# Stacking a query's high and low parts on the rows of one tile in a latent attention

## What is computed

```python
q = (q_lat @ w_qb).reshape(bsz, t_len, 6, 192)       # 128 plain and 64 rotated per head
q_pe, k_pe = rope_2d(q_pe, cos, sin), rope_2d(k_pe, cos, sin)
k_pe = jnp.broadcast_to(k_pe[:, :, None, :], (bsz, t_len, 6, 64))   # one rotated key for all heads
q, k = jnp.concatenate([q_nope, q_pe], -1), jnp.concatenate([k_nope, k_pe], -1)
s = jnp.einsum('bqhd,bkhd->bhqk', qblk, k) * 192 ** -0.5   # 128 queries against 256 + 512 keys
o = jnp.einsum('bhqk,bkhd->bqhd', jax.nn.softmax(s, axis=-1), v)
```

## Time and profile before

| | |
|---|---|
| median of 3 runs | 2432.0 us (2430.31 to 2433.66) |
| the profiled execution | 2423.83 us, span 2421.7 us |
| mean granted TensorE clock | 0.982 |
| TensorE (PE) busy | 2311.4 us, 95% of the span |
| weight loads (PEld) | 1932.8 us, 80% |
| VectorE (DVE) | 1170.0 us, 48% |
| ScalarE (ACT) | 868.9 us, 36% |
| GpSimd (POOL) | 974.8 us, 40% |
| slowest group of loads to land | 20.9 us (arena<-ada_dram, 768 KB each) |

### The profile page before, as it was taken

One profiled execution on the slowest core, in us unless ns is written; L12 is line 12 of the kernel. 1 busy time (PEld: TensorE's weight loads), 2 busy tenths in 40 slices (PEclk: granted clock), 3 DMA queues, 4 the chain that ended last, 5 costly groups with the idle time before them and its releaser, 6 DMA issues.

```text
span 2421.7 us, 36690 instructions
## 1 busy us (share of the span) xinstructions
PE 2311.4 (95%) x14013; PEld 1932.8 (80%) x14013; DVE 1170.0 (48%) x1873; ACT 868.9 (36%) x1399; POOL 974.8 (40%) x770
## 2 busy tenths in 40 slices
PE   6989989999999999999999999999999999999997
PEld 3878879888888888898877787778887886688766
DVE  4685681547777753343232346654232006670273
ACT  5444343341111122335224343222443225542452
POOL 2464563333333432333512145655664440154302
PEclk9989989999999999999999999999999999999999
DMA  7131232126555531112200024553223321122212
GB/s 287 66 115 69 72 122 84 53 93 203 183 196 191 184 104 61 61 61 91 64 1 1 18 87 156 183 197 110 98 89 116 97 87 47 55 76 90 66 45 70
DMA packets 64438, 245.11 MB, mean 101 GB/s; under 512 B 7168, under 2 KB 8448, under 8 KB 63552
## 3 DMA queue, kind: packets, MB, share of 16 engines
q1 hardware_dynamic: 64080, 242.67, 29.0%
q0 software_dynamic: 240, 0.79, 0.1%
HBM read 241.33 MB, written 2.10 MB: 101 GB/s over the span
## 4 chain that ended last, share of the span: by engine, by line
PE 73%; DVE 4%; issue 3%; ACT 3%; POOL 2%; DVEq 0%; POOLq 0%; ACTq 0%
PE ps L851 13%; PE ps L852 13%; PE ps L853 13%; PE ps L1554 4%; PE ps L1556 4%; PE ps L1557 4%; PE ps L612 2%; PE ps L1802 1%; PE ps L1789 1%; PE ps L1726 1%; POOL w_low L469 1%; PE ps L888 1%; PE ps L890 1%; PE ps L889 1%; ACT arena L2302 1%
## 5 line engine op out<-in xcount | busy, mean ns | idle before, releaser
L469 POOL TENSOR_TENSOR w_low<-ring,w_high 128x512 fp32r<-128x512 f32 (+2 forms) x534 | 752.0, 1430 | 1138.8 <-ACT w_high L460 1132.3
L460 ACT ACTIVATE w_high<-ring 128x1024 fp32r<-128x1024 f32 (+2 forms) x267 | 274.7, 1031 | 957.1 <-PE ps L853 638.8
L851 PE MATMUL ps<-h_high,w_high 128*128 128x512 f32 x1040 | 412.0, 396 | 17.1 <-POOL h_low L714 7.3
L852 PE MATMUL ps<-h_low,w_high 128*128 128x512 f32 x1040 | 407.4, 392 | 0.0
L853 PE MATMUL ps<-h_high,w_low 128*128 128x512 f32 x1040 | 407.0, 391 | 0.0
L851 PEld LDWEIGHTS ps<-h_high,w_high 128*128 128x128 f32 x1040 | 196.6, 189 | 70.9 <-issue 13.2
L853 PEld LDWEIGHTS ps<-h_high,w_low 128*128 128x128 f32 x1040 | 196.4, 189 | 41.7
L852 PEld LDWEIGHTS ps<-h_low,w_high 128*128 128x128 f32 x1040 | 196.8, 189 | 38.0
L2839 DVE TENSOR_TENSOR hidden<-arena,hidden 128x1536 fp32r<-128x1536 f32 (+1 forms) x42 | 87.2, 2077 | 193.3 <-ACT hidden L2098 193.3
L1554 PE MATMUL ps<-hidden,w_high 128*128 128x512 f32 (+1 forms) x504 | 178.6, 354 | 0.0
L1556 PE MATMUL ps<-hidden,w_high 128*128 128x512 f32 (+1 forms) x504 | 178.5, 354 | 0.0
(11 more groups left out here) (465 smaller groups left out, 4868.6 us busy)
## 6 DMA issues: line engine op xcount, KB each, us to landing
const<-late_w_dram SPq DMA_DIRECT2D x112, 512.0 KB, 5.0
ring<-up_dram SPq DMA_DIRECT2D x88, 512.0 KB, 3.3
ring<-down_dram SPq DMA_DIRECT2D x44, 512.0 KB, 3.2
ring<-winE_dram SPq DMA_DIRECT2D x32, 512.0 KB, 3.5
XB<-ada_dram SPq DMA_DIRECT2D x20, 768.0 KB, 5.4
ring<-win_dram SPq DMA_DIRECT2D x20, 512.0 KB, 3.2
ring<-winC_dram SPq DMA_DIRECT2D x20, 512.0 KB, 3.5
arena<-ada_dram SPq DMA_DIRECT2D x12, 768.0 KB, 20.9
```

Source lines behind the costliest of these rows:

```text
L460: nc.scalar.activation(WH[p][:, 0:L], RAW[p][:, 0:L], ACT.Copy).then_inc(w_hi, 1)
L469: ins = nc.gpsimd.tensor_tensor(WL[p][:, to], RAW[p][:, to], WH[p][:, to].bitcast(F32), ALU.subtract)
L851: nc.tensor.matmul(bank[:, 0:n], wh[:, cols], hi, start=(k == 0), stop=False)
L852: nc.tensor.matmul(bank[:, 0:n], wh[:, cols], lo, start=False, stop=False)
```

## The change

The high parts and the low parts of a head's rotated query (64 rows each) are put on the 128 rows of one tile, M_TS[h]: the head's own half of the rows holds the high part, the other half its low part. As the rotated key stands in both halves, one product of that tile with M_RH gives high x high + low x high, and a second with M_RL gives high x low (+ low x low, which was left out before). So `m_scores` issues two rotated products with 128 rows in place of three with 64.

To fill the tiles ScalarE copies the pair's rotated query whole into the first head's tile and its upper half into the second head's; GpSimd makes the low part in place over the query (M_TLOW stands where M_QP does), and SP moves each head's low half to the other half of the rows by a transfer from SBUF to SBUF, 64 rows of 2 KB. SP waits for GpSimd's count before each, and TensorE waits for the transfer (`rot_in[h]`) before each unit. SP issues these six after the first two loads of `woutM`; the other six loads follow.

```diff
--- before.py
+++ after.py
@@ -270,9 +270,10 @@
         M_KH = [parts(f"key_high{x}", at, T) for x, at in enumerate((ARENA_AT + 3072, ARENA_AT))]
         M_KL = [parts(f"key_low{x}", at, T) for x, at in enumerate((H_AT + 3072, ARENA_AT + T))]
         M_RH, M_RL = (parts(f"key_rot{x}", ARENA_AT + 24320 + x * T, T) for x in range(2))
-        M_TH, M_TL = ([parts(f"query_rot{x}{j}", at, S) for j, at in enumerate(ats)] for x, ats in enumerate((
-            (H_AT + KT * S, H_AT + KT * S + 2 * S, ARENA_AT + 24320 + 2 * T),
-            (H_AT + KT * S + S, H_AT + KT * S + 3 * S, ARENA_AT + 24320 - 2 * S))))
+        M_TS = [parts(f"query_rot{h}", at, S) for h, at in enumerate((
+            H_AT + KT * S, H_AT + KT * S + S, H_AT + KT * S + 2 * S, H_AT + KT * S + 3 * S,
+            ARENA_AT + 24320 + 2 * T, ARENA_AT + 24320 - 2 * S))]
+        M_TLOW = [parts(f"query_rot_low{x}", ARENA_AT + 11 * S + 3 * T + x * S, S) for x in range(3)]
         GS = parts("hidden", H_AT, 2, 2, 2, T)
         G1 = [(parts("hidden_first0", ARENA_AT + 32 * T, 2, T), SQR.rearrange("p k n -> p (k n)")[:, 0:2 * T].rearrange("p (k n) -> p k n", k=2)),
               [parts(f"hidden_first1{x}", ARENA_AT + 22 * S + x * 2 * S, 2, S) for x in range(2)]]
@@ -1099,9 +1100,10 @@
                 return M_KN[:, x, :], M_KH[x % 2], M_KL[x % 2]
             if what == "q":
                 return M_QN[:, x, :], SQR[:, 2 * (x % 2), :], SQR[:, 2 * (x % 2) + 1, :]
-            return M_QP[:, x, :], M_TH[x], M_TL[x]
+            return M_QP[:, x, :], M_TS[2 * x:2 * x + 2], M_TLOW[x]
 
         m_tab = sem("m_tab")
+        rot_in = [sem(f"rot_in{h}") for h in range(HEADS_M)]
         m_dft = sem("m_dft")
         m_rope = sem("m_rope")
         m_max = sem("m_max")
@@ -1305,7 +1307,14 @@
                 if stage in LATER:
                     load_up(stage)
                     continue
-                first = 2 if stage in ("woutE", "woutC") else 0
+                first = 2 if stage in ("woutE", "woutC", "woutM") else 0
+                if stage == "woutM":
+                    for k in range(2):
+                        load_split(sp, stage, k, k)
+                    for h in range(HEADS_M):
+                        sp.wait_ge(qk_lo, M_PARTED.index(("t", h // 2)) + 1)
+                        mine, other = slice(64 * (h % 2), 64 * (h % 2) + 64), slice(64 - 64 * (h % 2), 128 - 64 * (h % 2))
+                        sp.dma_start(M_TS[h][other, :].bitcast(F32), M_TLOW[h // 2][mine, :].bitcast(F32)).then_inc(rot_in[h], 16)
                 if stage == "winE":
                     with sp.Fori(0, 4) as i:
                         for k in range(2):
@@ -1693,21 +1702,19 @@
                 h, i = units[u]
                 b = bank_use("mS", u)[0]
                 open_bank(pe, "mS", u)
-                o = 64 * (h % 2)
                 pe.wait_ge(qk_lo, max(M_PARTED.index(x) for x in (("q", h), ("t", h // 2))) + 1)
+                pe.wait_ge(rot_in[h], 16)
                 _, kh, kl = m_parts("k", h)
                 _, qh, ql = (x[:, i * P:(i + 1) * P] for x in m_parts("q", h))
-                _, th, tl = (x[o:o + 64, i * P:(i + 1) * P] for x in m_parts("t", h // 2))
-                rh, rl = M_RH[o:o + 64, :], M_RL[o:o + 64, :]
+                both = M_TS[h][:, i * P:(i + 1) * P]
                 MM = nc.tensor.matmul
                 for j, (a, n) in enumerate(SEGS):
                     to = ps[:, b + j, 0:n]
                     MM(to, qh, kh[:, a:a + n], start=True, stop=False)
                     MM(to, ql, kh[:, a:a + n], start=False, stop=False)
                     MM(to, qh, kl[:, a:a + n], start=False, stop=False)
-                    MM(to, th, rh[:, a:a + n], start=False, stop=False)
-                    MM(to, tl, rh[:, a:a + n], start=False, stop=False)
-                    ins = MM(to, th, rl[:, a:a + n], start=False, stop=True)
+                    MM(to, both, M_RH[:, a:a + n], start=False, stop=False)
+                    ins = MM(to, both, M_RL[:, a:a + n], start=False, stop=True)
                 sums_done(ins, "mS", u)
 
             def m_turn(u):
@@ -2235,7 +2242,11 @@
                             await_sums(act, "mS", 4 * x - 5)
                         await_taken(act, *spread_sum("nqk", 10 + 2 * x if what == "k" else x))
                     whole, high, _ = m_parts(what, x)
-                    A(high, whole, ACT.Copy).then_inc(qk_hi, 1)
+                    if what == "t":
+                        A(high[0], whole, ACT.Copy)
+                        A(high[1][64:128, :], whole[64:128, :], ACT.Copy).then_inc(qk_hi, 1)
+                    else:
+                        A(high, whole, ACT.Copy).then_inc(qk_hi, 1)
 
             part_keys(0, 4)
             for u in range(26):
@@ -2461,6 +2472,7 @@
                     for x in range(len(M_PARTED)):
                         whole, high, low_ = m_parts(*M_PARTED[x])
                         pool.wait_ge(qk_hi, x + 1)
+                        high = high[0] if M_PARTED[x][0] == "t" else high
                         TT(low_, whole, high.bitcast(F32), ALU.subtract).then_inc(qk_lo, 1)
                     continue
                 if stage[:4] == "down":
```

## The result

The changed kernel took 2402.2 us (median of 4 runs, 2399.4 to 2409.6) against 2432.4 us before (4 runs): ratio 0.988, 95% interval 0.986 to 0.990. In more rounds on one chip it took 2403.4 us (6 runs) against 2430.4 (17 runs): ratio 0.989, interval 0.9865 to 0.9915. So it is faster by 27 to 30 us, and by somewhat more than the range of the forecast, 2405 to 2418, allowed.

The account below looks back on a forecast made before the run. TensorE's queue was taken to bound the 24 units: 24 x 0.99 = 23.8 us (8.6 removed product, 15.1 gaps) less 2.7 for stalls at the start gives 21.1 off the 2432.0 median: 2411 us, range 2405 to 2418.

Parts of the forecast that it names:

- The gaps: TensorE's scores: 0.63 us a unit lost at four places where 128-row and 64-row products meet; all go, 15.1 us.
- The added wait: TensorE's wait for the transfer before each unit: 0 to 0.07 us each, 0 to 1.7 in all, taken as 0.
- The three stalls at the start: TensorE waits of 0.6, 0.9 and 1.2 us in the first units, sum 2.7 us given back once.
- (a): Rival: the gaps in the scores aren't the change of shape; 7.6 us less, 2424; 6 in 100.
- (b): Rival: stalls at the start let TensorE's clock fall, costing 0.9 to 1.8 us, 2413; 8 in 100.
- (c): Rival: TensorE no longer bounds the steady part, ScalarE's round does; 6 us, 2417; 9 in 100.
- (d): Rival: slower, as head 0's transfer lands late before the first score product; 2439 if it takes 40 us; 2 in 100.
- New scores: 1.87 us, 0.99 less: Score products of one unit on TensorE after the change: 1.87 us instead of 2.86; over 24 units 23.8 us.
- the 0.08 in front of the transposes: Fourth gap, from the last score product (L1710) to the transposes: 0.20 us for 0.12, counted within the 0.63 us.
- I take the saving off the median: Last step: 21.1 us taken off the timed runs' median 2432.0, though the profiled execution took 2423.8; gives 2411.
- spread of the runs (1.7 to either side): Run-to-run spread added to the bounds 2406.5 and 2416.7 to give the range 2405 to 2418.
- the clock as a rival: Rival (b): the changed kernel's stalls at the start lower the clock, costing 0.9 to 1.8 us; 8 in 100.

Follow-up runs that it names:

- shape alone: Three rotated products as in the kernel before the change, but all with 128 rows (the third repeats the second): 2411.4 us, ratio 0.9935 against that kernel.

## Why the forecast missed

The parts that were right, by its own steps. The gaps belong to the change of shape (shape alone). The products that stay take no longer with 128 rows. SP, GpSimd and the transfers cost nothing, with 1253.1 for the first low half, as against 1253.2, and a landing in 2.4 us. The added wait cost nothing in the stage and 0.1 us in front of it. The three stalls at the start were forecast as 0.6, 0.9 and 1.2 and are 0.71, 0.91 and 1.17. Rivals (a), (b), (c) and (d) did not happen; the stalls at the start left the clock at 1.00.

**A term too small.** "New scores: 1.87 us, 0.99 less" is 1.84 and 1.02: the plain step with 512 columns is 0.23, not the 0.24 that I read from one unit. And I named the 0.08 in front of the transposes as a gap but took back no gain in the transposes' own first step; it is 0.06. So 25.9 (24 x 1.08) less 2.8 is 23.1, and measured 22.7, where I had 23.8 less 2.7, 21.1. Most of the 0.4 between lies behind the start of the last unit, where the changed kernel gains 0.9 us instead of 1.2.

**The step that failed** is the last one, "I take the saving off the median", with its "spread of the runs (1.7 to either side)". It made the saving of one undisturbed profile the saving of every execution. The term that it put at nothing is what the 64-row form in head 0 costs in executions where the clock falls: 8.9 us of the stage in the one profile of the kernel before that had it, and 2.5 to 8.3 us on the average by the kernel with the form in heads 1 to 5 alone. The profile I worked from had no fall, so the sum could not contain it; the change takes it away. With it 22.7 becomes 25 to 31, which holds the 27 and 30 measured. For all of that the fall would have to come in three to nine executions of ten; the one profile of four that had it is at the low end, and by it alone (2.2 us) the saving would be 25. I had the clock as a rival in one direction only, as something that the change could worsen.

The 1.7 to either side was too little as well. That the profile lay 8.2 below the median I noted and did not follow up. The three later profiles of the kernel before took 4.9, 15.2 and 14.7 us more than it (2428.7, 2439.0 and 2438.5), and of that 5, 5 and 15 us lie outside the stage, in low-clock stretches that both kernels have. So a part of the miss is chance: the ratio of the larger number of rounds puts the changed kernel at 2405.6 from the same 2432.4, just inside the range, and its interval allows a saving of 21 to 33 us.

"TensorEngine Tiling (Array Packing)", section "Key Properties", in the Trainium skill, says that a change of the tiling mode drains TensorE. The runs agree: 0.68 us a unit for four changes of shape, 0.17 each on the average. The rule of "TensorE: Matmul & The Clock Gate", section "Step-by-step: what each phase is for", in the Trainium skill, that weight loads are pulled ahead, shows here between products of one shape only. In the kernel before, in the unit of the earlier trace rows, the weight loads (PEld) of a product behind one of its own shape (L1707, L1710) and of two behind a change (L1708, L1705):

```profile
1299.62 0.19 PEld L1707 LDWEIGHTS ps<-key_low,squares_rounded 128*128 128x128 f32 x1
1300.17 0.18 PEld L1708 LDWEIGHTS ps<-key_rot,query_rot 64*128 64x128 f32 x1 [0.37 <-issue]
1300.51 0.18 PEld L1710 LDWEIGHTS ps<-key_rot,query_rot 64*128 64x128 f32 x1
1301.06 0.19 PEld L1705 LDWEIGHTS ps<-key_high,squares_rounded 128*128 128x128 f32 x1 [0.36 <-issue]
```

The first and third start 0.23 and 0.24 us ahead of their products, the other two with them, in all 24 units. Whether a drained engine holds the load back, or the load that comes late is itself the gap, no run here separates.

## What to carry to other kernels

A group of products that contract 64 rows in a stream of 128-row ones costs two changes of shape beside its own time, some 0.34 us here: lay the starts of neighbouring products side by side, and where the odd ones can share a full-height tile, a product is saved and the changes too. A stream that TensorE fills completely can still hold such gaps, for they are counted as busy (113.21 of 113.21 us before). Compare kernels by the length of the changed stage, which repeated here to 0.02 us where the clock stayed up, and not by one profile against a median. If the profile is shorter than the runs by a good part of the expected saving, take more profiles before the forecast: a cost that only some executions have, such as the fall here, is in none of the rows of one that lacks it.

## What the runs showed that I had not expected

TensorE's clock fell from 2.4 to 1.2 GHz while the engine was busy: it had done 13.9 us of 128-row products of 32-bit floats, stood idle for 1.41 or 1.51 us and then issued a few 64-row products among 128-row ones. Some 2 us after the first of the scores the clock was at 0.50, and it stayed there for 14 to 20 us in which the engine was busy all through. It happened in five of eight profiles with that form in the first units, and in none of six with 128 rows in the same units, though those stalled two or three times for 0.2 to 1.2 us soon after. And the fulfilled waits: three more in front of each of 24 units changed the stage by 0.01 us, while in front of unit 0, where TensorE was waiting, they went with 0.17 us.
